# A two-block transformer kernel: four of sixteen rows of the modulation matrix on TensorE, weights loaded first, and another order around the second norm and the expert transition

## What is computed

```python
# first block: modulation, three attention branches, SwiGLU
mod = silu(c) @ w_ada + b_ada                      # [2048] @ [2048, 12288]
shift1, scale1, gate1, shift2, scale2, gate2 = split(mod, 6)
h = rms_norm(x, norm1_gain) * (1 + scale1) + shift1
x = x + gate1 * mixing_sublayer(h, ...)            # h @ w_in, branches, w_out
h = rms_norm(x, norm2_gain) * (1 + scale2) + shift2
x = x + gate2 * swiglu(h, w_ffn_in, w_ffn_out)
# second block
h = x + mixer(rms_norm(x, mix_norm))
hn = rms_norm(h, ffn_norm)
h = h + hierarchical_moe(hn)    # best of 4 groups, best 2 of its 8 experts, 32 experts in all
h = h + sigmoid(rms_norm(h, ple_norm) @ w_ple_gate) * (p @ w_ple_up)
```

## Time and profile before

| what | value |
|---|---|
| median of 3 runs | 2930.59 us (2930.58 to 2933.04) |
| the profiled execution, its own time | 2932.33 us |
| its span, first to last instruction | 2930.2 us |
| mean granted TensorE clock | 0.982 of full |
| PE busy | 2811.2 us (96%) |
| DVE busy | 1938.9 us (66%) |
| ACT busy | 1480.0 us (51%) |

### The profile page before, as it was taken

One profiled execution on the slowest core, in us unless ns is written; L12 is line 12 of the kernel. 1 busy time (PEld: TensorE's weight loads), 2 busy tenths in 40 slices (PEclk: granted clock), 3 DMA queues, 4 the chain that ended last, 5 costly groups with the idle time before them and its releaser, 6 DMA issues.

```text
span 2930.2 us, 37397 instructions
## 1 busy us (share of the span) xinstructions
PE 2811.2 (96%) x12693; PEld 2295.0 (78%) x12693; DVE 1938.9 (66%) x2223; ACT 1480.0 (51%) x1825; POOL 16.6 (1%) x27
## 2 busy tenths in 40 slices
PE   3699999999999899999999999999899999999999
PEld 2587877788887688888888888788778887878787
DVE  6867866677777655555554565766555458989884
ACT  3356454444444454344434456544454447777773
POOL 0000000000000000000000000000000000000000
PEclk9799999999999899999999999999999999999999
DMA  9967877678887556556666565555245569999984
GB/s 332 363 216 225 278 231 242 200 243 282 283 282 273 167 175 202 191 178 201 192 190 191 187 195 147 154 158 180 91 176 186 191 209 358 362 359 361 360 290 137
DMA packets 347808, 676.95 MB, mean 231 GB/s; under 512 B 24280, under 2 KB 114832, under 8 KB 347168
## 3 DMA queue, kind: packets, MB, share of 16 engines
q1 hardware_dynamic: 346048, 669.29, 68.8%
q0 software_dynamic: 1632, 5.95, 0.7%
HBM read 673.04 MB, written 2.10 MB: 230 GB/s over the span
## 4 chain that ended last, share of the span: by engine, by line
PE 88%; DVE 6%; ACT 3%; issue 2%; DMA 0%; ACTq 0%; DVEq 0%
PE bank L751 27%; PE bank L753 27%; PE bank L752 27%; DVE big L2161 2%; DVE wlo L2206 1%; PE bank L831 1%; PE bank L780 1%; DVE wlo L2076 0%; PE bank L1310 0%; ACT whi L1443 0%; PE bank L1136 0%; ACT whi L1430 0%; PE bank L1008 0%; DMA raw<-in_w_in 0%; PE bank L1359 0%
## 5 line engine op out<-in xcount | busy, mean ns | idle before, releaser
L751 PE MATMUL bank<-whi,ahi 128*128 128x512 f32 x2400 | 960.5, 400 | 48.1 <-DVE wlo L2206 27.8
L753 PE MATMUL bank<-whi,alo 128*128 128x512 f32 x2400 | 943.5, 393 | 0.0
L752 PE MATMUL bank<-wlo,ahi 128*128 128x512 f32 x2400 | 943.1, 393 | 0.0
L2064 DVE TENSOR_TENSOR wlo<-raw,whi 128x1024 fp32r<-128x1024 f32 x540 | 652.5, 1223 | 401.2 <-ACT whi L1437 396.0
L1437 ACT ACTIVATE whi<-raw 128x1024 fp32r<-128x1024 f32 x540 | 566.6, 1059 | 455.0 <-PE bank L753 395.7
L751 PEld LDWEIGHTS bank<-whi,ahi 128*128 128x128 f32 x2400 | 456.1, 190 | 150.8 <-issue 36.4
L753 PEld LDWEIGHTS bank<-whi,alo 128*128 128x128 f32 x2400 | 455.7, 190 | 97.9
L752 PEld LDWEIGHTS bank<-wlo,ahi 128*128 128x128 f32 x2400 | 456.4, 190 | 92.1 <-issue 0.7
L2206 DVE TENSOR_TENSOR wlo<-raw,whi 128x1024 fp32r<-128x1024 f32 x280 | 341.0, 1222 | 203.6 <-ACT whi L1430 201.3
L1430 ACT ACTIVATE whi<-raw 128x1024 fp32r<-128x1024 f32 x280 | 294.9, 1059 | 319.0 <-PE bank L753 255.3
L751 PE MATMUL bank<-whi,bhi 128*128 128x512 f32 x944 | 370.7, 393 | 0.0
(11 more groups left out here) (487 smaller groups left out, 1748.1 us busy)
## 6 DMA issues: line engine op xcount, KB each, us to landing
raw<-in_w_in SPq DMA_DIRECT2D x296, 512.0 KB, 4.4
raw<-in_w_ada SPq DMA_DIRECT2D x192, 512.0 KB, 5.2
raw<-in_w_ffn_in SPq DMA_DIRECT2D x352, 256.0 KB, 3.4
raw<-in_w_expert_gate SPq DMA_DIRECT2D x128, 512.0 KB, 4.9
raw<-in_w_expert_up SPq DMA_DIRECT2D x128, 512.0 KB, 5.8
raw<-in_w_expert_down SPq DMA_DIRECT2D x128, 512.0 KB, 6.3
raw<-in_w_ffn_out SPq DMA_DIRECT2D x88, 512.0 KB, 4.2
raw<-in_w_out SPq DMA_DIRECT2D x64, 512.0 KB, 4.8
```

The source lines that it names most:

```text
L751: mm(o, shi[:, kc, T], whi[:, s, c], start=st, stop=False)
L752: mm(o, shi[:, kc, T], wlo[:, s, c], start=False, stop=False)
L753: ins = mm(o, slo[:, kc, T], whi[:, s, c], start=False, stop=en)
L2064: V.tensor_tensor(wlo[:, t % 4], raw[:, t % 8], whi[:, t % 4].bitcast(F32), ALU.subtract)\
```

## The change

It does three things, all by the order of instructions and by which engine does them. First, SP issues the vector c, the identity and eight tiles of `w_ada` ahead of the other small vectors, POOL loads x at once, silu(c) comes from a transpose of its own, and the barrier `stage_end` goes. DVE does 12 of the 16 row tiles of a part (`DVE_ROWS`), and PE does the last four straight from `raw`, one set each, in `lead_columns`; `lead_store(part)` now stands at the end of its own part. Second, around the second norm, ACT's copies of the gate, the load of the root's table and the gained pieces are moved, and the second pair of gate quarters goes ahead of L1120. Third, in the expert transition, the routing weights are worked out between the gathered chunks, `slot_is` comes before the order of experts, and `token_turn` comes after the up products of round 0.

```diff
+        DVE_ROWS, PE_ROWS = 12, 4
...
-            sp.dma_start(ident[:], I["consts"][:, C_ID:C_ID + P]).then_inc(S("small_landed"), 16)
+            sp.dma_start(c_rows, r1("c", 16)).then_inc(S("stored"), 16)
+            sp.dma_start(ident[:], I["consts"][:, C_ID:C_ID + P]).then_inc(S("stored"), 16)
+            for k in range(8):
+                load(k, ada_part(0, k))
...
-            sp.dma_start(xres[:], I["x"].rearrange("(b p) n -> p b n", p=P)).then_inc(S("x_landed"), 16)
...
-            wait_stage(pool, ST_LOAD)
+            fetch("x_landed", xres[:], I["x"].rearrange("(b p) n -> p b n", p=P))
...
+            def lead_columns(part):
+
+                tiles = [i for i, is_product in enumerate(PART_ORDER) if not is_product]
+                at = (lambda k: k) if part == 0 else (lambda k: lead_tile(part, tiles[k]))
+                pe.wait_ge(S("mod_done"), part + 2)
+                pe.wait_ge(lo_ready, at(DVE_ROWS - 1) + 1)
+                for j in range(8):
+                    mm(bank[6][:, j:j + 1], acc[:, part % 2, j * P:(j + 1) * P], ones[:, 0:1], start=(j == 0), stop=False)
+                for k in range(DVE_ROWS, 16):
+                    t = at(k)
+                    w = raw[:, t % 8].rearrange("p a n -> p (a n)")
+                    pe.wait_ge(landed[t % 8], 16 * (t // 8 + 1))
+                    for j in range(8):
+                        ins = mm(bank[6][:, j:j + 1], w[:, j * P:(j + 1) * P], silu_c[:, k:k + 1], start=False, stop=(k == 15 and j == 7))
+                    ins.then_inc(S("ada_cols" if k == 15 else "ada_pe"), 1)
...
             for part in range(1, ADA_PARTS):
-                pe.wait_ge(S("norm_lo"), 2 * part)
                 seen = 0
                 for i, is_product in enumerate(PART_ORDER):
                     if is_product:
+                        pe.wait_ge(S("norm_lo"), 2 * part - 1 + seen % 2)
                         lead_product(lead_tile(part, i), part - 1, seen)
                         seen += 1
-                ada_columns(lead_tile(part + 1, 0), part, acc[:, part % 2])
-            pe.wait_ge(S("norm_lo"), 8)
+                lead_columns(part)
             for i in range(6):
+                pe.wait_ge(S("norm_lo"), 7 + i % 2)
                 lead_product(t_last + i, 3, i)
...
             late_turn("n2", 3)
-            pe.wait_ge(S("gate_gd"), DC + 10)
+            gate_broadcast("g2", (2, 3), 2 * DC)
+            pe.wait_ge(S("gate_gd"), 2 * DC + 2)
...
-                    if rnd == 0 and k == 2:
-                        token_turn()
...
                 if rnd == 0:
+                    token_turn()
                     slot_weights()
...
-                                           item(18): lambda g, par: gate_broadcast("g2", (0, 1)),
-                                           item(19): out1_seen(1), item(24): out1_gained(1), item(27): out1_seen(2),
-                                           49: out1_gained(2), 51: out1_seen(3)}, ffn_first, prologue=False, single=True)
+                                           item(19): out1_seen(1), item(22): lambda g, par: gate_broadcast("g2", (0, 1)),
+                                           item(24): out1_gained(1), item(27): out1_seen(2),
+                                           51: out1_last}, ffn_first, prologue=False, single=True)
             late_squares("n2", 3)
+            late_root("n2")
             gained(3)
-            late_root("n2")
+            gate_broadcast("g2", (2, 3))
             for j in range(8):
                 shifted_hi(j)
-            gate_broadcast("g2", (2, 3))
...
             def lead_store(part):
 
+                for i in range(PE_ROWS - 1):
+                    dve.wait_ge(S("ada_pe"), (PE_ROWS - 1) * part + i + 1)
+                    dve.sem_inc(lo_ready, 1)
                 dve.wait_ge(S("ada_cols"), part + 1)
+                dve.sem_inc(lo_ready, 1)
...
-            for k in range(16):
+            for k in range(DVE_ROWS):
                 ada_rows(k, 0, k, acc[:, 0])
-                if k == 6:
+                if k == 2:
+                    dve.wait_ge(S("vec_T"), 2)
+                    V.tensor_copy(vec[:], bank[0][:, 0:V_ALL]).then_inc(S("vec_cols"), 1)
+                if k == 5:
                     dve.wait_ge(S("norm_ss"), 2)
...
-                if k == 8:
+                if k == 6:
                     dve.wait_ge(S("norm_std"), 1)
                     V.reciprocal(stat[:, 6:8], stat[:, 4:6]).then_inc(S("x_scale"), 1)
+            dve.wait_ge(S("vec_cols"), 1)
+            lead_store(0)
...
-                    else:
+                    elif i - seen < DVE_ROWS:
                         ada_rows(t, 0, i - seen, acc[:, part % 2])
-                    if i == 1:
-                        lead_store(part - 1)
-                    if i in (4, 5):
-                        lead_lo(part - 1, i - 4)
-            lead_store(3)
+                    if i in (2, 3):
+                        lead_lo(part - 1, i - 2)
+                lead_store(part)
...
-                if j == 4:
-                    gate_diag("g2", modt[:, 80:96], range(8, DC))
...
             V.tensor_tensor(rt[:, 40:42], m2, m1, ALU.subtract).then_inc(S("rt_dif"), 1)
+            for k in range(8):
+                gathered_lo(k)
             dve.wait_ge(S("rt_exp"), 2)
...
             V.tensor_tensor(wlarge, w8, wide(in_large, 8), ALU.mult).then_inc(moe_dve, 1)
+            for k in range(8, DC):
+                gathered_lo(k)
```

More of the change, by code:

```diff
@@ L406, in lead_src @@
                 return in_src(2 * part + i % 2, (i // 2) * COLS)
-            for k in range(16):
+            for k in range(8, 16):
                 load(k, ada_part(0, k))
@@ L1515, in gate_broadcast @@
                 for q in quarters:
-                    act.wait_ge(S("gate_gb"), 4 * (GATE_NO[key] - 1) + q + (2 if key == "g2" and q >= 2 else 1))
+                    act.wait_ge(S("gate_gb"), 4 * (GATE_NO[key] - 1) + q + 1)
                     A(gate_bc[key][:, q * COLS:(q + 1) * COLS], bank[6 + q % 2][:], ACT.Copy).then_inc(S("gate_bc"), 1)
@@ L1522, in side_turn @@
                 act.wait_ge(S("side_done"), no)
-            act.wait_ge(S("vec_cols"), 1)
-            A(silu_c[:], vec[:, V_C:V_C + 16], ACT.Silu).then_inc(S("silu_c"), 1)
-            stage_end(act, "act")
+            act.wait_ge(S("ones_set"), 4)
+            act.wait_ge(S("vec_T"), 1)
+            A(silu_c[:], bank[1][:, 0:DC], ACT.Silu).then_inc(S("silu_c"), 1)
+            A(rows[:, 8:9], ones[:, 0:1], ACT.Sqrt)
             act.wait_ge(S("x_landed"), 16)
@@ L1963, in row_high @@
                 A(x_hi[:, b], xres[:, b], ACT.Identity, scale=rstd[:, b:b + 1]).then_inc(moe_act, 1)
+            side_turn(3, 36)
             row_high(0)
-            side_turn(3, 36)
             row_high(1)
+            act.wait_ge(S("rt_sub"), 1)
+            A(rt[:, 0:8], rt[:, 0:8], ACT.Exp).then_inc(S("rt_exp"), 1)
             for k in range(DC):
@@ L1969, in _ @@
                 A(ghi[:, k], bank[k % 8][:, 0:SLOTS], ACT.Identity, scale=gain_ffn2[:, k:k + 1]).then_inc(moe_act, 1)
+                if k == 7:
+                    act.wait_ge(S("rt_dif"), 1)
+                    A(rt[:, 40:42], rt[:, 40:42], ACT.Exp).then_inc(S("rt_exp"), 1)
                 if k >= 9 and k % 2 == 1:
                     split_moe(t_moe + (k - 9) // 2, 0)
-            act.wait_ge(S("rt_sub"), 1)
-            A(rt[:, 0:8], rt[:, 0:8], ACT.Exp).then_inc(S("rt_exp"), 1)
-            act.wait_ge(S("rt_dif"), 1)
-            A(rt[:, 40:42], rt[:, 40:42], ACT.Exp).then_inc(S("rt_exp"), 1)
-            act.wait_ge(moe_pe, PE_TOKENS)
-            for j in range(2):
-                A(token_of[:, j], bank[6][:, j * 256:(j + 1) * 256], ACT.Copy).then_inc(moe_act, 1)
             def moe_out_hi(rnd, g):
@@ L2016, in moe_round @@
                         follow(i - 32)
+                    if rnd == 0 and i == 6:
+                        act.wait_ge(moe_pe, PE_TOKENS)
+                        for j in range(2):
+                            A(token_of[:, j], bank[6][:, j * 256:(j + 1) * 256], ACT.Copy).then_inc(moe_act, 1)
                     if i % 8 == 3 and i > 8:
@@ L2520, in out1_store @@
                 ada_store(11, 88)
+                dve.wait_ge(S("mod_done"), 14)
+                gate_diag("g2", modt[:, 80:96], range(8, DC))
             def out1_gain(g, par):
@@ L2533, in _ @@
                     .then_inc(S("gate_gd"), 1)
-            dve.wait_ge(S("gate_gb"), 7)
+            dve.wait_ge(S("gate_gb"), 9)
             scaled(0)
@@ L2826, in _ @@
                     .then_inc(moe_dve, 1)
+            past, order = rt[:, 332:336], rt[:, 336:340]
+            step(V.tensor_scalar(past, tab(M_REST, 4), large, None, ALU.is_ge))
+            step(V.scalar_tensor_tensor(order, past, 8.0, tab(M_REST8, 4), ALU.mult, ALU.add))
+            step(V.tensor_scalar(order[:, 0:1], large, 32.0, 8.0, ALU.add, ALU.mult))
+            V.tensor_copy(first_expert[:], order).then_inc(moe_dve, 1)
```

(2 more changed lines are left out.)

54 lines of the change are left out of this document (18 added, 36 removed).

## The result

The changed kernel takes **2965.05 us** (median of 4 runs, 2961.83 to 2966.83) against 2931.28 for the kernel before in 4 runs: a ratio of 1.0114, with a 95% interval of 1.0098 to 1.013. It is slower. The profiled execution has 2966.83 us and a span of 2965.1, 34.9 more than the span before. The forecast sum was 2966.4 for the own time and 2964 for the median.

The account below looks back on a forecast made before the run. PE, busy 96% of the span, was taken as the bound. Lead +49.7, second norm -10.3 and expert transition -5.3 gave +34.1 on 2932.33, so 2966.4 us, or 2964 as a median; range 2936 to 2975.

Parts of the forecast that it names:

- the likeliest case: Whole kernel: the clock falls during PE's sets, for a median of 2964 us; chance 0.57.
- The lead: Everything before the first product behind part 3: ends 49.7 us later with the falling clock, 27.7 with a full one.
- second norm: Around the second norm: gate copy -2.4, gate broadcast's wait and half clock -9.15, pair ahead of L1120 +1.3; sum -10.3 us.
- expert transition: Up to and in expert round 0: 2.95 us of wait, 1.7 clock, 0.4 in front, 0.25 gaps; sum -5.3 us.
- Start: Start of the lead: transfers some 6.6 us earlier, of which 2.2 remain, so columns start at 39.4 instead of 41.63.
- Cycle: Each part of the lead: 39.0 us at full clock instead of 30.77, with 5.5 more if the clock falls.
- gain 0: Part 0 of the lead: its gain comes at 49.85 instead of 44.80 at full clock, 5.5 later if the clock falls.
- What the clock cost: PE's sets in the lead: a falling clock adds 5.5 us four times, +22.0, to the 27.7 at full clock.
- Falling clock: PE's sets in the lead: full clock lasts 3.1 us, so five sets take 15.2 us instead of 9.75; chance 0.57.
- Transfer-bound: Rival on the lead: the cycle stays 30.77 and everything ends earlier, -24.1 us, 2906.5; chance 0.06.
- the changes to the norms do nothing: Rival: stalls at 1005 and 2143 move to the next wait, 15.6 us return, 2980 or 2958; chance 0.12 with more lost.

Follow-up runs that it names:

- e11_start_only: Kernel before plus the norm changes and the changed start (early transfers), with the parts as before: 2919.44 us.
- e10_dense: Changed kernel plus three 128x512 matmuls, results unread, behind every column of the sets on tiles in parts 1 to 3: 3016.81 us in one run.
- e3_expert: Kernel before plus only the edits of the expert transition: 2926.18 us, ratio 0.9981.
- e4_norm_expert: Kernel before plus the edits of the second norm and the expert transition, lead as before: 2916.45 us, ratio 0.9946.
- e6_warm: Changed kernel plus one 128x512 matmul, result unread, behind every second column of the sets on tiles in parts 1 to 3: 2985.1 us, ratio 1.0183.

## Why the prediction was right

The sign, the likeliest case and the size came out: a forecast of 2964 against 2965.05 measured. That it came so near is luck in part, since the errors of the terms cancel. The lead has +49.70 (forecast +49.7), the second norm -11.17 (-10.3), the expert transition -4.69 (-5.3), and the end +1.1, for which the forecast had no term. Step by step:

- **Start: wrong.** The sets of part 0 were to begin at 39.4, and began at 42.29. The step that failed is "DVE waits for them behind its third row tile, till about 23.1": it waited until 25.33, 2.2 us longer. SP had issued the eight tiles only by 11.4 us and the last of the small vectors by 19.7. The whole 2.2 us that I credited to the early transfers are gone, and `e11_start_only` shows the same with the parts of before. The other 0.7 us came with slower transposes, for which I had no term.
- **Cycle: right, each piece within 0.7 us.** In part 1, gain to first product 10.22 us (10.1 forecast), products 17.93 (18.6, because the clock came back after 3 us and not 5), sets 14.91 (15.2), the rest 0.66 (0.55). Together 43.7 against 44.5, and 43.5 as the mean of three parts. Three times 1.0 less cancels the 2.9 us by which gain 0 was later than forecast (58.28 against 49.85 + 5.5), so that the +49.7 for the lead was met to the tenth by errors of opposite sign.
- **What the clock cost.** From their start to 0.66 us ahead of the gain, the sets take 15.33, 14.91, 14.45 and 13.97 us in parts 0 to 3, 58.7 in all; at 1.95 for each of the twenty it would be 39.0. So by this estimate 19.7 us of the 49.7 are the clock and 30.0 the order and the number of the sets. The forecast had 22.0 and 27.7.
- **Falling clock: right.** Of the rivals this one was weighed most, and the windows decide it; `e10_dense` shows that the same sets hold full clock when large matmuls stand between them. The Trainium skill, TensorE: Matmul & The Clock Gate, What's actually happening, says that the gate follows how busy PE has been. The windows have PE busy 2.00 of 2.00 us at 0.50, so busy in the sense of the profile's column isn't it; the measurement decides.
- **Second norm: right.** -2.36 (forecast -2.4), +1.16 (+1.3), and -9.97 (-9.15): the 22nd product also gained 0.9 us ahead of the broadcast's old place, as PE came back to full clock sooner (1037.99 - 1034.27 = 3.7 us behind its first product, where it was 991.03 - 985.77 = 5.3). PE had done the broadcast shortly before; that this is the reason wasn't tried.
- **Expert transition: right in sum.** I forecast -0.4 for the first product and it was +0.80. The step that failed is "`slot_is` comes 1.2 us earlier". Counted from PE's transposes of the last quarter it comes after 2150.24 - 2137.00 = 13.24 us, where it was 2111.37 - 2098.54 = 12.83. Two things held it back: the wait for `bhi`, and PE's twelve matmuls for the routing at 2140, at a granted clock of 0.50 and 0.41 us each, where before they had 0.28. In `e3_expert` these twelve have 0.28, `slot_is` comes after 12.01 us and the first product after 30.10 instead of 30.43, near the forecast. The rest was -5.49, of which 0.7 comes back with `token_turn`.
- **Rivals.** Transfer-bound was excluded by the cycle of 43.5. That the changes to the norms do nothing was excluded by `e4_norm_expert`.

Neither the wait for `bhi` nor the half clock of the routing matmuls was tried apart; both are read from the traces. Of the 1.1 us of the last step, the 0.4 beyond `token_turn` stay open.

## What to carry to other kernels

Work that moves to the engine that sets the end has to be cheap there and overlap something. Here 5.5 us of DVE's work in a part became 13 us of PE's, in series with everything, and DVE spent what it had saved waiting in the store. An early load is worth only what its first consumer does with it: put the steps that release the next engine ahead of a wait for something that they don't need. And when several edits go in together, cut them apart: here two of three were worth 0.5%, and the third hid them.

## What the hardware showed that I hadn't expected

PE's clock falls to half while PE is busy without a gap. One-column passes do it, and still do with a 128x512 matmul behind every second column (0.50 from 92 us on in `e6_warm`). With three behind every column it dips once in a part and then stays at 1.00 (`e10_dense`). The sets of part 1 cost 14.9 us for 80 passes, 0.19 a pass on the mean, where a set in a run of products has 1.95 / 16 = 0.12.
